# Two column blocks of the indexer's projection put into one, and the index scores and selection rounds moved

## What is computed

```
proj = n @ w_in
(qa, ka, va, iq, ik, iw, qb, kb, vb, g_low, og) = _split(proj, AB_SIZES)
...
iq = rope_partial(iq.reshape(bsz, s_len, IDX_HEADS, IDX_DIM), pos)
ik = rope_partial(ik[:, :, None, :], pos)[:, :, 0, :]
oa = dsa_attention(qa, ka, va, iq, ik, iw).reshape(bsz, s_len, A_WIDTH)
...
gate = (g_low @ w_gate_up + b_gate).astype(jnp.float32)
...
ob = gla_chunked(qb, kb, vb, lg).astype(n.dtype)
```

## Time and profile before

| | us |
|---|---|
| median of three runs | 1617.66 (1616.68 to 1617.95) |
| the profiled execution, its own time | 1617.04 |
| its span in the trace | 1614.90 |
| PE busy in the span | 1602.2 (99%) |
| DVE, ACT, POOL busy | 877.0, 606.8, 315.0 |
| index, first matmul of block 0 to the head weights' transposes | 386.71 to 433.26 |
| gla and dsa, from there to the first whole-width projection behind them | 433.26 to 622.73 |

### The profile page before, as it was taken

One profiled execution on the slowest core, in us unless ns is written; L12 is line 12 of the kernel. 1 busy time (PEld: TensorE's weight loads), 2 busy tenths in 40 slices (PEclk: granted clock), 3 DMA queues, 4 the chain that ended last, 5 costly groups with the idle time before them and its releaser, 6 DMA issues.

```text
span 1614.9 us, 20370 instructions
## 1 busy us (share of the span) xinstructions
PE 1602.2 (99%) x7736; PEld 1318.3 (82%) x7736; DVE 877.0 (54%) x1189; ACT 606.8 (38%) x844; POOL 315.0 (20%) x337
## 2 busy tenths in 40 slices
PE   9999999999999999999999999999999999999999
PEld 7888787787778997888888888878887888888887
DVE  7435554565779975453433344567876533434342
ACT  6323332325254565431222123467674321222121
POOL 0001111014246442220101012332233200101010
PEclk9999999999999999999999999999999999999999
DMA  7222222222212221222322222221212223222222
GB/s 240 82 101 78 78 93 88 93 81 102 79 53 71 73 80 53 93 91 105 103 85 99 104 85 98 78 84 74 79 53 72 86 104 104 99 84 104 104 78 105
DMA packets 25782, 145.90 MB, mean 90 GB/s; under 512 B 3936, under 2 KB 5616, under 8 KB 9200
## 3 DMA queue, kind: packets, MB, share of 16 engines
q1 hardware_dynamic: 25712, 144.93, 25.6%
HBM read 142.83 MB, written 2.10 MB: 90 GB/s over the span
## 4 chain that ended last, share of the span: by engine, by line
PE 88%; DVE 10%; ACT 1%; issue 1%; POOL 0%; DVEq 0%; ACTq 0%; POOLq 0%
PE ps_G L474 27%; PE ps_G L476 26%; PE ps_G L475 26%; DVE wide L2127 1%; DVE top L2123 1%; PE ps_AV L913 1%; PE ps_C L560 1%; DVE wide L2312 1%; PE ps_C L574 1%; PE ps_C L659 1%; PE ps_AV L686 1%; DVE wl L1756 1%; PE ps_C L913 1%; PE ps_C L755 1%; PE ps_C L474 0%
## 5 line engine op out<-in xcount | busy, mean ns | idle before, releaser
L474 PE MATMUL ps_G<-nh,wh 128*128 128x512 f32 x1016 | 398.9, 393 | 0.4 <-DVE h L2029 0.2
L476 PE MATMUL ps_G<-nh,wl 128*128 128x512 f32 x1016 | 395.5, 389 | 0.0
L475 PE MATMUL ps_G<-nl,wh 128*128 128x512 f32 x1016 | 395.4, 389 | 0.0
L1090 ACT ACTIVATE wh<-raw 128x2048 fp32r<-128x2048 f32 x126 | 240.5, 1909 | 324.1 <-PE ps_G L476 309.1
L474 PE MATMUL ps_G<-ch,wh 128*128 128x512 f32 x832 | 332.2, 399 | 0.0
L1756 DVE TENSOR_TENSOR wl<-raw,wh 128x2048 fp32r<-128x2048 f32 x112 | 259.3, 2316 | 128.6 <-ACT wh L1090 125.5
L475 PE MATMUL ps_G<-cl,wh 128*128 128x512 f32 x832 | 324.6, 390 | 0.0
L476 PE MATMUL ps_G<-ch,wl 128*128 128x512 f32 x832 | 324.6, 390 | 0.0
L474 PEld LDWEIGHTS ps_G<-nh,wh 128*128 128x128 f32 x1016 | 190.7, 188 | 45.4 <-issue 5.5
L476 PEld LDWEIGHTS ps_G<-nh,wl 128*128 128x128 f32 x1016 | 190.7, 188 | 40.0
L475 PEld LDWEIGHTS ps_G<-nl,wh 128*128 128x128 f32 x1016 | 190.8, 188 | 39.9 <-issue 1.0
(11 more groups left out here) (362 smaller groups left out, 1716.1 us busy)
## 6 DMA issues: line engine op xcount, KB each, us to landing
raw<-wst SPq DMA_DIRECT2D x129, 1024.0 KB, 4.8
raw<-wst SPq DMA_DIRECT2D x8, 256.0 KB, 6.1
outT<-h SPq DMA_DIRECT2D x8, 256.0 KB, 2.0
h<-xT SPq DMA_DIRECT2D x7, 256.0 KB, 6.5
raw<-wst SPq DMA_DIRECT2D x2, 512.0 KB, 5.7
tabs<-rb_d SPq DMA_DIRECT2D x1, 1024.0 KB, 7.8
tabs<-tab_d SPq DMA_DIRECT2D x1, 512.0 KB, 3.5
h<-xT SPq DMA_DIRECT2D x2, 128.0 KB, 3.3
```

The source lines that it names most:

```text
L474: mm(o, ah, bh, start=first, stop=False)
L475: mm(o, ah, bl, start=False, stop=False)
L476: return mm(o, al, bh, start=False, stop=last)
L1090: A(wh[s][:], raw[s][:], ACT.Copy).then_inc(w_hi, 1)
```

## The change

- The six blocks of index become five. `kz`, a new first block (bank C2), holds the head weights in rows 0 to 7, the gate's rank in rows 32 to 47 and the key once, in rows 64 to 127. The four query blocks follow. The tiles stay three; the last half tile is zeros and is not split.
- The key is written to both halves of the partitions by a new float32 matmul with 64 rows (`twice`, bank C0), and swapped for its rotation by another (`perm`, "key"), in place of the perm of the old block 4. Both, and the head weights' transposes (now bank C1), come behind the first query block. Their 64x256 constants come by a new DMA of 64 KB. DVE multiplies the key by cosine and sine itself; POOL's `rope_cos` goes from 5 to 4.
- The perm of the last query block moves into the middle of gla's block 0; the gate's product no longer waits for the head weights.
- ACT splits half of index's third tile, then gla's first two tiles as soon as their buffers are free, the second of them ahead of the wait for `rope_out`.
- `AFTER[0]` grows from three index scores to five; the later ones move forward by two, and none is left behind block 5.
- Selection rounds move forward. In gla p = 0 they were 14 for tile 1 and 4 for tile 2; now 16 and 5. In gla p = 1 tile 1 goes from 2 to 0, tile 2 from 6 to 9, tile 3 from 8 to 9.
- In the first group of stick the low part of the third tile is made in two halves, one ahead of `apply(1)` and one inside it.

```diff
-          ("index", 1, 3, 6), ("gla", 2, 3, 6), ...
+          ("index", 1, 3, 4), ("gla", 2, 3, 6), ...
...
-        MIDWAY = ((), (3, 4), (7, 8), (11, 12), (15, 16), (19, 20, 21))
-        AFTER = ((0, 1, 2), (5, 6), (9, 10), (13, 14), (17, 18), (22, 23))
+        MIDWAY = ((), (5, 6), (9, 10), (13, 14), (17, 18), (21, 22, 23))
+        AFTER = ((0, 1, 2, 3, 4), (7, 8), (11, 12), (15, 16), (19, 20), ())
...
+            need_tile(st, 0)
+            take(("kz",))
+            s, each = st.slot(0), fed_by(2)
+            for c in range(KC):
+                each(c)
+                ins = three(bank_of(("kz",))[:], wh[s][:, c, 0:P], wl[s][:, c, 0:P], mh[:, c, :], ml[:, c, :],
+                            c == 0, c == KC - 1)
+            ins.then_inc(done[use[("kz",)][0]], 1)
+            for k in range(4):
+                if k % 2:
+                    need_tile(st, (k + 1) // 2)
+                project(st, k, (k + 1) // 2, (k + 1) % 2 * P, mh, ml)
+                if k == 0:
                     token_scales(2, fb[:, 1, :], 2)
-                if k:
+                    settled(pe, ("kz",))
+                    pe.wait_ge(twice_in, 16)
+                    for key, x in ((("perm", "key"), twice_swapped), (("twice",), twice)):
+                        take(key)
+                        mm(bank_of(key)[:], x, wide[64:128, 15, :], start=True, stop=True).then_inc(
+                            done[use[key][0]], 1)
...
+                else:
                     perm(k - 1, tmp[:, 2 + (k - 1) % 2, :])
...
-                    stands(pe, Step("index", 0), 5)
...
+                    settled(pe, ("kz",))
                     take(("gate", p))
...
+                        if p == k == 0 and c == KC // 2:
+                            perm(3, tmp[:, 3, :])
...
-            split(st, 1)
-            split(st, 2)
+            s = st.slot(2)
+            act.wait_ge(raw_full[s], st.tile_use(2) * 16 + 16)
+            ready_block(st, 0)
+            A(wh[s][:, :, 0:P], raw[s][:, :, 0:P], ACT.Copy).then_inc(w_hi, 1)
+            s = st.slot(3)
+            act.wait_ge(raw_full[s], st.tile_use(3) * 16 + 16)
+            ready_block(st, 2)
+            A(wh[s][:], raw[s][:], ACT.Copy).then_inc(w_hi, 1)
...
                 if p == 0:
+                    split(st, 0)
                     act.wait_ge(rope_out, 5)
-                if p == 0:
-                    split(st, 0)
...
-                    select(*(((0, 0, 0), (0, 0, 0), (6, 0, 0), (2, 0, 0), (0, 0, 0), (2, 2, 0)),
-                             ((0, 0, 1), (0, 1, 1), (0, 1, 1), (2, 1, 0), (0, 2, 2), (0, 1, 2)))[p][k])
+                    select(*(((0, 0, 0), (3, 0, 0), (4, 0, 0), (3, 0, 0), (0, 0, 0), (2, 3, 0)),
+                             ((0, 1, 1), (0, 1, 1), (0, 1, 1), (0, 2, 1), (0, 2, 2), (0, 2, 2)))[p][k])
...
-                    choose(0, 1, 1)
+                    choose(0, 0, 1)
...
-                    choose(0, 3, 3)
+                    choose(0, 1, 2)
...
-                    choose(0, 1, 1)
+                    choose(0, 0, 1)
...
-                    apply(1)
-                    split(st, 1)
+                    split_part(st, 1, 0)
+                    apply(1, lambda: split_part(st, 1, 1))
```

More of the change, by code:

```diff
@@ L42 @@
 STAGES = [("values", 1, 4, 4), ("gates", 2, 2, 4), ("mix1", 4, 4, 8), ("join1", 2, 2, 8), ("out1", 2, 2, 4),
-          ("index", 1, 3, 6), ("gla", 2, 3, 6), ("dsa", 2, 3, 6), ("outab", 2, 2, 4),
+          ("index", 1, 3, 4), ("gla", 2, 3, 6), ("dsa", 2, 3, 6), ("outab", 2, 2, 4),
           ("ffn0", 4, 8, 16), ("stick", 4, 3, 6), ("outc", 2, 2, 4), ("ffn1", 4, 8, 16)]
@@ L275, in build @@
         book("AV", ("rt", 2))
-        for r in range(5):
+        book("C2", ("kz",))
+        book("C0", ("twice",))
+        book("C1", ("iw",))
+        for r in ("key", 0, 1, 2, 3):
             book("SX", ("perm", r))
-        book("SX", ("iw",))
         for p in range(2):
             book("SX", ("gate", p))
-            for n in (range(17) if p == 0 else ()):
+            for n in (range(19) if p == 0 else ()):
                 book(f"C{n % 3}", ("idx", n))
@@ L284, in build @@
             if p == 0:
-                for n in range(17, 19):
+                for n in range(19, 21):
                     book(f"C{n % 3}", ("idx", n))
@@ L293, in build @@
             if p == 0:
-                for n in range(19, 24):
+                for n in range(21, 24):
                     book(f"C{n % 3}", ("idx", n))
@@ L740, in _ @@
             st = Step("index", 0)
-            for k in range(6):
-                if k % 2 == 0:
-                    need_tile(st, k // 2)
-                project(st, k, k // 2, (k % 2) * P, mh, ml, each=fed_by(2) if k == 0 else None)
-                if k == 1:
-                    token_scales(2, fb[:, 1, :], 2)
-                if k:
+            need_tile(st, 0)
[11 more added lines that the diff above has]
+                if k == 0:
+                    token_scales(2, fb[:, 1, :], 2)
+                    settled(pe, ("kz",))
[4 more added lines that the diff above has]
+                            done[use[key][0]], 1)
+                    take(("iw",))
+                    for t in range(NT):
+                        last = nc.tensor.transpose(bank_of(("iw",))[:, t * 8:t * 8 + 8],
+                                                   wide[0:8, 15, t * P:(t + 1) * P], ident[0:8, 0:8])
+                    last.then_inc(done[use[("iw",)][0]], 1)
+                else:
                     perm(k - 1, tmp[:, 2 + (k - 1) % 2, :])
@@ L766, in gate_products @@
                 def gate_products(p):
-                    stands(pe, Step("index", 0), 5)
-                    if p == 0:
-                        take(("iw",))
-                        for t in range(NT):
-                            last = nc.tensor.transpose(ps["SX"][:, t * 8:t * 8 + 8],
-                                                       wide[0:8, 15, t * P:(t + 1) * P], ident[0:8, 0:8])
-                        last.then_inc(done["SX"], 1)
+                    settled(pe, ("kz",))
                     take(("gate", p))
@@ L1637, in _ @@
             pool.wait_ge(tables_in, 32)
-            for r in range(5):
+            for r in range(4):
                 rope_cos(r, tabI[0], tmp[:, r % 2, :])
@@ L2058, in _ @@
             r2 = fb[:, 1, :]
-            for k in range(6):
-                if k % 2 == 0:
+            for k in range(5):
+                if k == 2:
+                    s = st.slot(2)
+                    dve.wait_ge(w_hi, st.tile(2) + 1)
+                    tt(wl[s][:, :, 0:P], raw[s][:, :, 0:P], wh[s][:, :, 0:P].bitcast(F), ALU.subtract).then_inc(w_lo, 1)
+                elif k % 2 == 0:
                     split(st, k // 2)
@@ L2539, in constants @@
     tok = np.stack([ca[0:32].T, sa[0:32].T * sign]).reshape(2, NT, P, 32)
-    return small, np.concatenate([earlier, reset], 1), np.stack([ci, si]), np.ascontiguousarray(tok.transpose(2, 0, 1, 3).reshape(P, -1))
+    twice = np.concatenate([np.eye(64, dtype=np.float32)] * 2 + [pi[0:64, 0:64]] * 2, 1)
+    return (small, np.concatenate([earlier, reset], 1), np.stack([ci, si]),
+            np.ascontiguousarray(tok.transpose(2, 0, 1, 3).reshape(P, -1)), twice)
 def kernel(**inputs):
@@ L2547 @@
     x = {k: np.asarray(a) for k, a in inputs.items()}
-    small, mask, tables, turning = constants()
+    small, mask, tables, turning, twice = constants()
     near = np.minimum(P + np.arange(P)[:, None] - np.arange(2 * P)[None, :], P) + P
```

53 lines of the change are left out of this document (33 added, 20 removed).

## The result

The changed kernel takes **1619.34 us** (median of 20 runs, 1618.60 to 1621.62) against 1617.10 of the kernel before beside it (20 runs, 1616.08 to 1618.21): ratio 1.0014, 95% interval [1.0008, 1.0020]. Its profiled execution took 1619.50 us with a span of 1617.5; that of before was 1617.04 with 1614.9. So the change costs 2.2 us. The forecast was 1616.5, from 0.9 us less on the profiled execution, where 2.5 more were measured. The result lies inside the stated range and inside the 0.2% that the prediction took as the least it could tell, but the whole interval is on the slow side, where a small gain was forecast.

What follows compares the result with a forecast made beforehand. PE was taken as the bound, with DVE close behind over index and gla. Net +0.6 us behind dsa and -1.5 in stick gave -0.9, forecast 1616.5 us, 8-in-10 range 1612.8 to 1620.5.

Steps and rivals of the forecast that it cites:

- a second tile in a round: DVE in gla p = 1: choosing for a second tile in one selection round adds 1.0 us.
- +1.9 us at the upright products: At dsa's first upright products (L896): PE, waiting for DVE's rotated queries, resumes 0.4 + 1.5 = 1.9 us later than before.
- the slow rival: Rival, chance 0.15: three clock falls instead of one over 400 to 444 us, giving 1620.7, or 1621.6 with DVE late.
- The price of a fall: PE over 436 to 440 us: one fall of the granted clock cost 4 x 0.43 = 1.7 us before.
- PE's queue in index: Index up to the gate: block -5.45, 64-row product +0.96, head weights' wait -0.36, sum -4.85 us for PE alone.
- DVE's work beside POOL: Index: four DVE operations beside POOL's early split take 0.4 us more each, 1.6 together; gate's product at 430.95.
- The stand at the fourth score: Behind gla's gate: PE stands 2.0 us before the fourth score, waiting for ACT's relu of the first.
- The stand of 1.3 us in the middle of block 1: Gla: PE stands about 1.3 us for the third and fourth relu, which wait for DVE's first two adds.
- The 13.7 us from the gate to block 2: Gla: block 2 begins 13.7 us behind the gate's product, at 444.65; before it was 444.89.
- First turns: In dsa: fewer rounds there leave DVE and POOL ready, so the first turns shrink from 2.33 to 1.01 us, -1.3.
- Stick: Stick's first group: PE's 1.4 us wait for DVE's low part goes; -1.5 us, bounds -1.0 and -1.6.
- The saving stays: Rival, chance 0.28: POOL's split does not slow DVE and gla's idle times swallow the extra rounds; 1612.6 us.

## Why the prediction was right or wrong

It was wrong in sign: -0.9 us forecast on the profiled execution, +2.5 measured. One term was mis-sized. Out of it came a stand and a low clock at a place for which the sum had nothing. The other terms held to within 0.4 us.

- **The term that failed: the rounds in p = 1.** I priced "a second tile in a round" at +1.0 us, the difference of two durations. The round itself did cost 1.04. But it pushed the output of p = 0's second head from beside POOL's split onto POOL's two products, and that cost 1.5 more; the run with one round back shows 2.5 us for it. I had the rows of this contention in hand and used them for index only. With 2.5 in place of 1.0 the "+1.9 us at the upright products" would have been 3.4; DVE was ready there 562.34 - 559.24 = 3.1 us later than before.
- **The wait's place.** I expected DVE's lateness to appear at dsa's upright products alone and never compared DVE's release with PE's arrival at the output products of p = 1. In before PE started there 2.47 us behind the start of DVE's last masked product, when the first one is done (527.98 and 525.51); a standing PE starts 0.07 behind it (528.96 and 528.89), so the slack was 2.4. DVE came 3.4 us later (528.89) and PE would have come 0.36 earlier (528.96 - 1.34 = 527.62): 3.38 + 0.36 - 2.40 = 1.34, the wait measured. Without the 1.5 us of contention this is below zero: no stand. The two scores taken out of `AFTER[5]`, which I booked as lost in the wait, are part of that. So PE did not wait at the upright products, which I had named as the sign that my reckoning of the rounds is wrong.
- **The clock.** I had the slow rival at 400 to 444 us, and there nothing new happened (0.57 as before, in the profiled execution). It fell at 531 to 542 us instead, behind the new stand and in front of the small output products. The sum had nothing for the clock there. It adds 564.16 - 562.34 = 1.8 us at the upright products to what DVE's lateness costs anyway. Together: 3.1 + 1.8 = 4.9 instead of 1.9, 3.0 of the 3.4 us by which the sum was off. The rest is the stick edit, 0.4 short in this trace. The price of a fall, 1.7 us, was too high as well: it came from one trace of before, and two later traces of the same code up to there (the stick edit alone and the rounds alone) had 1.00 over 436 to 440 and reached gla's third block only 0.7 us sooner behind the gate (10.1 us instead of 10.9).
- **PE's queue in index:** right. 0.96 for the 64 rows; the head weights' wait is gone; the gate at 431.39 against 430.95 forecast. The 0.4 are DVE's work beside POOL. For it I had 1.6 us; against the run with the late split it was 2.0 (two pairs of scalings 3.03 and 2.26 us instead of 2.55 and 1.41, two additions 1.05 and 1.00 instead of 0.69). The Trainium skill (SBUF — State Buffer, Summary: rules for kernel authors) goes further than what I cited of it: of a DVE operation with two SBUF inputs and a GpSimd operation that reads SBUF, the one that is issued second is blocked until the first is done. The traces agree in size: a pair of scalings grows by 2.54 - 1.41 = 1.13 us beside one POOL product of 1.3 us.
- **The stand at the fourth score:** right to the hundredth (2.0 and 2.03), and from its cause: the run with three scores does not have it. The stand of 1.3 us in the middle of block 1 did not appear, because the half clock ahead of it brought PE there late; at full clock it was 0.67. I had counted on this cover and added only 0.3 us for the clock. The 13.7 us from the gate to block 2 (the terms named add up to 13.4) were 13.72 with the stand filled and 14.05 in the changed kernel, so the 0.3 fits this trace. That is luck: in five of the six other traces with a stand of 2.0 to 2.5 us there it was 15.1 to 15.5.
- **First turns:** right, -1.3 (1.01 us instead of 2.33). **Stick:** -1.5 forecast, -1.45 by the medians of the run that has it alone and -1.1 by the waits, inside its bounds of -1.0 and -1.6.
- **"The saving stays"** was right for the projections: the gate's 2.6 us reach the end in full (-2.9). It failed for the change as a whole, because the rounds were in it.

## What to carry to other kernels

Cost an operation that is moved forward by what it pushes, not by its own duration: write down for each operation behind it which operation of the neighbouring engine it will lie beside, and compare each later release with the consumer's arrival, product by product. Where a stand and a low clock follow one another, or a low clock and a wait, do not add them: fill the one in thought and see whether the other takes its place. Between two engines that disturb each other, first try another order on the engine that is late; here that was worth 1.9 us, while moving the neighbour's work away was worth nothing, since it held up ACT instead. And look at more than one trace before you price a low clock: the one that I read was not what the same code did in two others.

## What the runs showed of the hardware

- **Granted clock.** At the output products of p = 1 two traces have a stand of PE (1.34 and 2.48 us), followed by small products. Behind it the clock was at half rate (1.2 instead of 2.4 GHz), from about 532 to 542 us and from about 531 to 544. In the eleven traces without a stand there, and in the one with the stand filled by 1.55 us of products, it stayed at 1.00. At the scores it was alike: behind a stand of 2.0 to 2.5 us the clock over 436 to 440 was 0.50 to 0.64 in all seven traces, and 1.00 where the fill left only 0.55 us of the stand. A long stand isn't needed for it, though: of the six traces with three scores and no such stand, the kernel before had 0.57 there behind small products and a wait of 0.36, while two others with the same products and a wait of 0.35 had 1.00. The Trainium skill (TensorE: Matmul & The Clock Gate, A second HAM failure mode: psum-queue depth-cycling) tells of a kernel in which short idle times of PE between groups of matmuls make the clock swing; these rows agree. How long the low stretch lasts differed between traces whose code up to there is the same: gla's third block started at 445.44 in the changed kernel and at 446.63 with the later rounds put back. What decides that stayed open.
- **DVE beside POOL.** A cast of 512 columns took 0.43 us alone, 0.84 beside POOL's split and 1.41 beside its product of 512 columns; the low part behind it 0.69, 1.09 and 1.67. Here POOL's single long products disturbed DVE more than its split, which is made of shorter ones.
